# Attention values projected straight into token-major form, with another order of the projection tiles

## The reference

```python
u = _rmsnorm(h, mix_norm[l])
p = u @ w_in[l]
rq, rk, rv, rg, dq, dk, dv = jnp.split(p, splits, axis=-1)
ret = _retention(rq, rk, rv, rg, ...)      # 4 heads of 128, decayed scores times v, then
                                           # (o - mean(o)) / sqrt(var(o)), times silu(rg)
dif = _diff_attn(dq, dk, dv, ...)          # 4 heads, softmax(0) - lam * softmax(1), times v,
                                           # then an rmsnorm over the 128 columns of the head
h = h + jnp.concatenate([ret, dif], axis=-1) @ w_out[l]
```

## Time and profile before

| | us |
|---|---|
| median of three runs | 1905.69 |
| lowest, highest | 1904.7, 1906.48 |
| the profiled execution | 1905.93 |
| its span, first to last instruction | 1903.3 |
| PE busy in it | 1884.6 |
| POOL, DVE, ACT busy | 1203.5, 1149.0, 914.2 |

### The profile page before, as it was taken

One profiled execution on the slowest core, in us unless ns is written; L12 is line 12 of the kernel. 1 busy time (PEld: TensorE's weight loads), 2 busy tenths in 40 slices (PEclk: granted clock), 3 DMA queues, 4 the chain that ended last, 5 costly groups with the idle time before them and its releaser, 6 DMA issues.

```text
span 1903.3 us, 29796 instructions
## 1 busy us (share of the span) xinstructions
PE 1884.6 (99%) x11578; PEld 1679.8 (88%) x11578; DVE 1149.0 (60%) x1875; ACT 914.2 (48%) x1462; POOL 1203.5 (63%) x812
## 2 busy tenths in 40 slices
PE   9999999999999999999999999999999999999997
PEld 7989989887888989989889898998788889899896
DVE  6727657438755744726676476663586367366276
ACT  7524535456425534524565254445564265255254
POOL 5857757455435867857468586765554277678582
PEclk9999999999999999999999999999999999999999
DMA  4333323232223232233234233223222133323231
GB/s 141 133 110 132 127 91 112 67 108 70 67 67 111 86 114 89 92 108 106 76 109 156 68 111 111 89 89 111 78 67 75 48 111 111 111 90 134 67 109 69
DMA packets 54999, 186.46 MB, mean 98 GB/s; under 512 B 6440, under 2 KB 7976, under 8 KB 54860
## 3 DMA queue, kind: packets, MB, share of 16 engines
q1 hardware_dynamic: 53136, 181.61, 28.4%
q10 hardware_dynamic: 1724, 2.96, 0.5%
HBM read 182.44 MB, written 3.15 MB: 98 GB/s over the span
## 4 chain that ended last, share of the span: by engine, by line
PE 85%; POOL 6%; DVE 4%; ACT 3%; issue 1%; DMA 1%; SPq 0%; DVEq 0%; ACTq 0%; POOLq 0%
PE bank L679 17%; PE bank L681 17%; PE bank L680 17%; PE pair L679 8%; PE pair L681 8%; PE pair L680 8%; POOL w_lo L586 1%; PE pair L929 1%; POOL w_lo L605 1%; PE pair L957 1%; PE bank L914 1%; PE bank L969 1%; POOL w_lo_x L605 1%; DVE bank L1485 1%; PE bank L719 1%
## 5 line engine op out<-in xcount | busy, mean ns | idle before, releaser
L577 POOL TENSOR_TENSOR w_lo<-raw,w_hi 128x512 fp32r<-128x512 f32 (+1 forms) x240 | 314.7, 1335 | 388.7 <-ACT w_hi L1036 388.7
L679 PE MATMUL bank<-hg_hi,w_hi 128*128 128x256 f32 (+1 forms) x1400 | 448.8, 321 | 0.0
L680 PE MATMUL bank<-hg_lo,w_hi 128*128 128x256 f32 (+1 forms) x1400 | 443.2, 317 | 0.0
L681 PE MATMUL bank<-hg_hi,w_lo 128*128 128x256 f32 (+1 forms) x1400 | 443.1, 317 | 0.0
L679 PEld LDWEIGHTS bank<-hg_hi,w_hi 128*128 128x128 f32 x1400 | 265.8, 190 | 21.1 <-issue 3.9
L680 PEld LDWEIGHTS bank<-hg_lo,w_hi 128*128 128x128 f32 x1400 | 266.0, 190 | 18.3 <-issue 1.2
L681 PEld LDWEIGHTS bank<-hg_hi,w_lo 128*128 128x128 f32 x1400 | 266.0, 190 | 17.7
L1036 ACT ACTIVATE w_hi<-raw 128x1024 fp32r<-128x1024 f32 (+1 forms) x120 | 124.1, 1034 | 262.3 <-PE bank L681 129.9
L1468 DVE SCALAR_TENSOR_TENSOR h<-pair,h 128x512 f32<-128x512 f32 x100 | 68.8, 689 | 250.2 <-PE pair L681 250.1
L679 PE MATMUL pair<-a_hi,w_hi 128*128 128x512 f32 x440 | 172.8, 393 | 1.9 <-issue 1.1
L681 PE MATMUL pair<-a_hi,w_lo 128*128 128x512 f32 x440 | 171.8, 390 | 0.0
(11 more groups left out here) (273 smaller groups left out, 4912.7 us busy)
## 6 DMA issues: line engine op xcount, KB each, us to landing
raw<-in_w_gu SPq DMA_DIRECT2D x96, 512.0 KB, 3.7
raw_x<-in_w_gu SPq DMA_DIRECT2D x80, 512.0 KB, 4.2
raw<-in_w_p SPq DMA_DIRECT2D x56, 512.0 KB, 3.4
raw_x<-in_w_dn SPq DMA_DIRECT2D x32, 512.0 KB, 3.7
raw<-in_w_dn SPq DMA_DIRECT2D x32, 512.0 KB, 3.6
raw<-in_w_o SPq DMA_DIRECT2D x16, 512.0 KB, 3.5
raw_x<-in_w_dn SPq DMA_DIRECT2D x16, 384.0 KB, 3.6
raw<-in_w_dn SPq DMA_DIRECT2D x16, 384.0 KB, 3.4
```

The costliest lines, as they stand in the source:

```text
L577: ins = pool.tensor_tensor(columns(lo_[:, part, :]), source[:, part.start * P:part.stop * P], columns(hi[:, part, :]).bitcast(F32), ALU.su ...
L679: pe.matmul(out, hi[:, 0, :], m_hi, start=first, stop=False)
L680: pe.matmul(out, hi[:, 0, :], m_lo, start=False, stop=False)
L681: return pe.matmul(out, lo_[:, 0, :], m_hi, start=False, stop=last)
```

## The change

A value tile is no longer formed with columns on the partitions. Two heads' values are formed as a pair in two steps (`value_product`): 128 tokens of `hg` are stationary and the weights of two heads, 256 columns, move. The first step does tokens 0 to 255, the second 256 to 511, each with 2 x 8 x 3 = 48 matmuls. Both steps need both heads' weights, so the first splits no new unit and the second splits two. ACT takes the result straight to `v` with a factor for each token (`take_values`: 2 instructions for dv, 4 for rv, these with row sums), and DVE removes the mean of rv one step later (`centre_values`, one instruction). The factor for each token comes from two new DVE instructions in step 1. PE's turnings and centring matmuls, DVE's take-over of values and ACT's copy of them are gone. The tile order and the steps of the scores are new. Attention's weights go through all four raw buffers, which `raw_x` now keeps for the whole program, and SP no longer waits for the output projection before it loads the second feed-forward block. The rest is bookkeeping of semaphores.

The new tile order is rg 0 to 3, dv0, dv1, dk0, dq0, dk1, dq1, dv2, dv3, dk2, dq2, dk3, dq3, rv0, rv1, rk0, rq0, rk1, rq1, rk2, rq2, rv2, rv3, rk3, rq3.

```diff
-            RAW_AT["e", E_ATT + _e] = _e % 2
+            RAW_AT["e", E_ATT + _e] = _e % (2 * RAW)
...
-TILES = ([("rg", h) for h in range(HEADS)] + [(k, h) for h in range(HEADS) for k in ("dk", "dq", "dv")]
-         + [(k, h) for h in range(HEADS) for k in ("rk", "rq", "rv")])
+TILES = [("rg", h) for h in range(HEADS)]
+for _h in (0, 2):
+    TILES += [("dv", _h), ("dv", _h + 1)] + [(k, h) for h in (_h, _h + 1) for k in ("dk", "dq")]
+TILES += ([("rv", 0), ("rv", 1)] + [(k, h) for h in range(3) for k in ("rk", "rq")]
+          + [("rv", 2), ("rv", 3), ("rk", 3), ("rq", 3)])
+VALUES = [t for t, tile in enumerate(TILES) if tile[0] in ("dv", "rv")]
+assert all(TILES[t][1] % 2 == t % 2 for t in VALUES)
+def first_value(t):
+    return t in VALUES and t % 2 == 0
+def second_value(t):
+    return t in VALUES and t % 2 == 1
...
-def scores_at(n): return 7 + 3 * (n // 2) + n % 2
+def scores_at(n): return (9, 10, 11, 12, 15, 16, 18, 19)[n]
...
-def ret_scores_at(h): return 19 + 3 * h
+def ret_scores_at(h): return (21, 23, 25, 28)[h]
...
+        raw_x = sb("raw_x", [P, RAW * UT * P])
...
-        centre = sb("centre", [P, P])
...
+        token_rms = sb("token_rms", [P, T // P])
+        value_sum = sb("value_sum", [P, 4])
...
-                    if c == 0 and f == 1:
-                        sp.wait_ge(h_ready, at(h_ready, l, len(CHUNKS) * KD + KD))
...
+                        if second_value(t):
+                            lo(l, E_ATT + AHEAD + t - 1)
+                        if not first_value(t):
+                            lo(l, E_ATT + AHEAD + t)
...
+            def value_product(l, t):
+                s = t % SLOTS // 2 * 2
+                for tt in (0, 1) if first_value(t) else (2, 3):
+                    out = proj[t][:, (tt % 2) * SEQ:(tt % 2 + 1) * SEQ].rearrange("p (a b) -> p a b", a=2)
+                    tokens = slice(tt * P, (tt + 1) * P)
+                    for k in range(KD):
+                        hi, lo_ = w_hi[:, s:s + 2, k, :], w_lo[:, s:s + 2, k, :]
+                        pe.matmul(out, hg_hi[:, k, tokens], hi, start=k == 0, stop=False)
+                        pe.matmul(out, hg_lo[:, k, tokens], hi, start=False, stop=False)
+                        last = pe.matmul(out, hg_hi[:, k, tokens], lo_, start=False, stop=k == KD - 1)
+                return last
...
-                        pe.wait_ge(lo_done, at(lo_done, l, E_ATT + t + 1))
+                        pe.wait_ge(lo_done, at(lo_done, l, E_ATT + t + 1 + first_value(t)))
                         if t >= 3:
-                            pe.wait_ge(proj_free, at(proj_free, l, t - 2 if t < 5 else t - 1))
-                        last = product(proj[t], s, hg_hi, hg_lo, KD)
+                            pe.wait_ge(*taken(l, t - 3 if t < 5 else t - 2))
+                        if t in VALUES:
+                            last = value_product(l, t)
+                        else:
+                            last = product(proj[t], s, hg_hi, hg_lo, KD)
...
+                        pe.wait_ge(value_taken, at(value_taken, l, hd_n // 2 * 2 + 2))
...
-                    if kind in ("dv", "rv"):
-                        use = VALUES.index((kind, hd))
-                        pe.wait_ge(proj_free, at(proj_free, l, t))
-                        if use:
-                            pe.wait_ge(value_free, at(value_free, l, use))
-                        if kind == "rv" and hd:
-                            pe.wait_ge(o_ret_free, at(o_ret_free, l, hd))
-                        for tt in range(T // P):
-                            value = values[:, tt * P:(tt + 1) * P]
-                            if kind == "dv":
-                                last = pe.transpose(o_ret[:, tt * P:(tt + 1) * P], value, ident[:, :])
-                            else:
-                                last = pe.matmul(o_ret[:, tt * P:(tt + 1) * P], value, centre[:, :], start=True,
-                                                 stop=True)
-                        last.then_inc(value_done, 1)
...
-                        pe.wait_ge(value_free, at(value_free, l, VALUES.index(("rv", hd_n)) + 1))
+                        pe.wait_ge(value_centred, at(value_centred, l, hd_n // 2 * 2 + 2))
+                        if hd_n:
+                            pe.wait_ge(o_ret_free, at(o_ret_free, l, hd_n))
...
+            def take_values(l, t):
+                kind, hd = TILES[t][0], TILES[t - t % 2][1]
+                if t == VALUES[0]:
+                    act.wait_ge(token_ready, at(token_ready, l, 1))
+                if kind == "rv":
+                    act.wait_ge(mixv_done, at(mixv_done, l, 2 * hd + 4))
+                    if VALUES.index(t) > HEADS:
+                        act.wait_ge(value_centred, at(value_centred, l, VALUES.index(t) - HEADS))
+                for tt in (0, 1) if first_value(t) else (2, 3):
+                    scale = token_rms[:, tt:tt + 1]
+                    at_ = (tt % 2) * SEQ
+                    if kind == "dv":
+                        ins = act.activation(flat(v[:, tt, hd:hd + 2, :]), proj[t][:, at_:at_ + SEQ], ACT.Copy, scale=scale)
+                    else:
+                        for j in range(2):
+                            i = 2 * (tt % 2) + j
+                            ins = act.activation(v[:, tt, hd + j, :], proj[t][:, at_ + j * P:at_ + (j + 1) * P], ACT.Copy,
+                                                 scale=scale, accum_out=value_sum[:, i:i + 1])
+                ins.then_inc(value_taken, 1)
...
+                        if second_value(t):
+                            split(l, E_ATT + AHEAD + t - 1)
+                        if not first_value(t):
+                            split(l, E_ATT + AHEAD + t)
+                        if t in VALUES:
+                            take_values(l, t)
...
-                    if kind in ("dv", "rv"):
-                        act.wait_ge(value_done, at(value_done, l, VALUES.index((kind, hd)) + 1))
-                        act.activation(v[:, :, hd, :], o_ret.rearrange("p (a b) -> p a b", b=P), ACT.Copy)\
-                            .then_inc(value_free, 1)
...
+                    if t - 1 in VALUES and TILES[t - 1][0] == "rv":
+                        centre_values(l, t - 1)
+                    if t < PROJ_TILES and t not in VALUES:
...
+                        spread = bass.AP(ident[:, :].tensor, ident[:, :].offset,
+                                         [list(ident[:, :].ap[0]), [0, T // P], [1, P]])
+                        diagonal = o_r[:, :].rearrange("p (a b) -> p a b", b=P)
+                        dve.tensor_tensor(diagonal, rms[:, :].rearrange("p (a b) -> p a b", b=P), spread, ALU.mult)\
+                            .then_inc(token_diag, 1)
+                        dve.wait_ge(token_diag, at(token_diag, l, 1))
+                        dve.tensor_reduce(token_rms[:, :], diagonal, AX.X, ALU.add).then_inc(token_ready, 1)
...
+                values = v[:, tt:tt + 2, hd:hd + 2, :]
+                dve.scalar_tensor_tensor(out=values, in0=spread, scalar=-1.0 / P, in1=values, op0=ALU.mult, op1=ALU.add)\
+                    .then_inc(value_centred, 1)
...
-                elif kind == "rg":
+                else:
                     dst = rg[:, hd, :]
-                else:
-                    if use := VALUES.index((kind, hd)):
-                        dve.wait_ge(value_done, at(value_done, l, use))
-                    dst = values[:, :]
```

42 lines of the change are left out of this document (23 added, 19 removed).

## The result

| | before | after |
|---|---|---|
| median of 17 runs each, us | 1905.74 | 1909.1 |
| lowest, highest | 1904.7, 1906.7 | 1908.2, 1909.78 |
| span of the profiled execution | 1903.3 | 1907.8 |

The ratio is 1.0017, 95% interval 1.0011 to 1.0024: 3.4 us slower, at a granted clock of 0.998 in both. PE is spared the work that it was to be spared, and loses a little more than that in new waits.

A forecast was written before the change was run, and what follows sets the result against it. PE was taken to bound the kernel. PE work of -10.3 + 4.5 = -5.8 us and new waits of +8.8 us gave +3.0, so 1908.7 us on the median, with a range of 1899.5 to 1914.5.

The forecast's parts named there:

- PE work removed: Value tiles' transposes (0.40 us each dv tile) and centring matmuls (0.89 each rv tile) go: 10.3 us, all on the path.
- PE work made dearer: Value pairs take 96 matmuls of 256 columns instead of 48 of 512: 4.5 us more over 8 pairs.
- Waits: New PE waits at four places in the attention loop: 4.4 us a layer, 8.8 us in two.
- A: Steps 12 to 14: PE waits 1.2 us for the statistic of dq2; bounds 0.5 and 1.6.
- B: Steps 18 and 19: PE waits 0.8 us to turn item 5, behind DVE's take-over, norm and weighting; bounds 0 and 2.
- C: Steps 20 and 21: PE waits 1.2 us for item 6, whose DVE weighting runs beside POOL; bounds 0 and 2.
- D: Steps 25 and 26: retention head 2's mixv waits 1.2 us for rv3's centring behind DVE's variance; bounds 0.7 and 2.
- E: Step 15, ahead of the statistic of head 0: a PE wait that the prediction did not list.
- What costs nothing: loading: Four raw buffers and SP's dropped wait start loads earlier, but win nothing, as PE is not waiting for loads.
- (1): Rival: the covers hold and all waits are gone, -5.8 us, 1899.9 us; chance 0.22.
- (2): Rival: DVE and POOL collide at all four places, waits of 7.6 us a layer, 1915.1 us; chance 0.33.
- (3): Rival: weight loads of narrow matmuls are not hidden, 59 us more, about 1965 us; chance 0.03.

The follow-up runs named there:

- one_block: Kernel before, with turning or centring of each value tile cut from four blocks to the first: 1897.47 us, ratio to before 0.9958.
- two_raw: Kernel after, with attention's weights through two raw buffers again and SP's wait for the output projection restored: 1911.59 us, ratio to before 1.0037.
- b_weighting_first: Kernel after, with DVE in step 18 doing item 5's weighting and item 6's bias and maximum ahead of head 1's norm: 1907.69 us, one run.
- all_five: Kernel after, five pieces moved earlier: POOL's square (step 13), DVE's weightings (18, 20), DVE's centring (25), ACT's dk3 factor (15): 1899.5 us, ratio to before 0.9970.
- d_centre_first: Kernel after, with DVE in step 25 centring rv3 ahead of the variance of retention head 1: 1906.61 us, one run.

## Why the prediction was right, and which steps of it were not

The forecast was 1908.7, the time is 1909.1. Step by step:

- **PE work removed, 10.3 us.** Right: 5.21 a layer, and one_block measured 8.2 us for the part of it worked out as 7.8.
- **PE work made dearer, 4.5 us.** Right: 2.26 a layer. The pace inside a pair is 0.120 us, not 0.119, which alone would make 0.64 for a pair and 5.1 in all; with the change-overs on both sides the sum over the block is 0.57. The gathered operand, which no row of before showed, costs next to nothing beside the contiguous one of the earlier trace rows (0.120 for 0.119). The estimate by the isolated gap in the Trainium skill (TensorE: Matmul & The Clock Gate, Back-to-back issue gap) was 1.0 us in all, which is far too low for these streams; the section itself says that the formula leaves out the weight loads and under-counts at small N.
- **Waits, 4.4 us a layer.** 4.38: A 1.18 (1.2 forecast), B 0.77 (0.8), C 1.20 (1.2), D 1.23 (1.2), each taken away by an edit of what was named as its cause. At B the terms held one by one: the take-over 2.89 (2.88), the norm's first instruction 1.78 (1.8), the weighting 1.86 (1.85). That the total fits to 0.1 us is in part luck all the same: the bounds given for B and C reached from 0 to 2 us, and which instruction meets which decides between such values, as two_raw (B 0.82 more, A 1.0 less) and b_weighting_first (C 0.27 more) show. At C the weighting ended 7.4 us after product 20, for which 7.5 was worked out by taking a row of before with POOL beside it and not one without.
- **A place passed over.** E, 0.21 us a layer. A gap at a place passed over was one of the prediction's own signs of being wrong, and this one came true. The layout followed the chain of each tensor but not the one bank of the statistics, which a factor on ACT holds. It is small here; once A is gone it is 0.5.
- **What costs nothing: loading.** "PE is not waiting for loads at the openings, so nothing is won" was a wrong step. Two units are split in one go behind each value pair. With two buffers the next transfers wait for POOL's subtractions of those two units, and a transfer lands 3.3 us after its issue (the page's median for two_raw); ACT then idles for 4.5 us ahead of the split for step 7 and 2.5 us ahead of the one for B (2.7 and 1.3 in the kernel after, there for PE). I had looked for waits of PE alone, and in the old order alone. The forecast was not hurt, because the layout of A to D took every split as never late, which only the four buffers make true. Without them the kernel is at 1911.6 to 1912.6, not at 1909.1.
- **PE busy to fall by about 6 us.** It fell by 3.1. Most of the difference is how busy time is counted: a matmul's length runs to its end, so each gap is preceded by about 0.17 us that looks busy, ten times in the two layers. In all_five, without the gaps, it fell by 4.6. The rest is not accounted for.
- **The signs in the trace.** The releasers at A, B and C are those named. At D the list showed "issue" and only d_centre_first named the centring.

Of the rivals, (1) is what all_five reaches; the case made against it, that A needs no contention, was wrong for A, whose chain holds a weighting beside POOL in step 12, from 442.20 to 446.95 or 4.75 us (the layout had taken over the 4.76 of the earlier trace rows). (2) had the right cause at C and B, where holding POOL back takes the waits away, and in part at A, but not its size: the four places make 4.38 us, where it needed 4.8 or more, with 7.6 at its end. (3) is refuted by the pace of 0.120.

## What to carry to other kernels

When PE sets the time, taking work from PE is worth its price only where every chain that was covered by that work has as much slack left. List the chains that end at PE within a step or two of the removed work, and move the last piece of each (the instruction that releases PE) ahead of its neighbours in the same edit: here that turned +3.4 us into -5.8. Judge two DVE chains beside POOL together, because a piece moved at one place meets POOL elsewhere at the next. And count slack for each unit of a pair when a change makes two transfers or splits come at once, also on engines that do not set the time.

## What the runs showed of the hardware

**DVE beside POOL loses by instruction, not by share.** Two scalings 0.74 us alone and 2.48 beside POOL, two subtractions 0.88 and 1.78 (2.81 in b_weighting_first), the norm's product 0.75 and 1.78, a cast 0.43 and 1.40, where POOL's two subtractions for a unit take 2.5 to 3.3 in place of 2.5. Which value it is depends on where the instruction falls: a start of POOL's unit 1.2 us later was enough to turn the cast's 0.43 into 1.40. In the C rows above the weighting ends at 511.37, 0.67 us after POOL's last subtraction (510.70), about 0.2 more than one subtraction needs by itself (0.88 for two). The Trainium skill (SBUF — State Buffer, Who interferes with whom) states that a DVE instruction with two SBUF inputs, or a copy, cast or scaling in its fast mode, contends with POOL and that the second one blocks until the first has ended. These rows agree with it, the scaling and the cast included; how long each was blocked can't be told from them.

**Narrow matmuls with a weight load each keep pace.** 128x256 products start every 0.120 us over 96 in a row, with a new stationary operand for every one of them and a load that takes 0.19 us. By columns that is 6% dearer than the 128x512 ones at 0.227.
